# A decoder layer on one core: rows of empty expert slots left out, one result row per token and choice, longer weight runs, another order of the gate product, and a combine without gathers

## The chip, the cores and the metric

The kernel runs on one core of a Trainium2 chip. Its engines are TensorE (PE, with its weight loads as PEld), VectorE (DVE), ScalarE (ACT), GpSimd (POOL) and SyncE (SP). SP, ACT and POOL each issue DMAs on a queue of their own, and the packets of all queues share 16 DMA engines. The metric is the device time of one execution in microseconds (us), the median of several.

## The reference

One layer of a decoder for 1,024 prompt tokens and 32 sample tokens (8 sequences of 4), D = 1024, everything in float32: a mixer (attention and retention) that the change touches in two small places only, then a mixture of experts, then a last normalization. The part that matters, cut short:

```python
def hierarchical_moe(xn, ...):
    ...
    # top group of 4, then the two best of its 8 experts: 2 choices a token
    y = grouped_expert_mlp(xf, experts, gates, w_gate, w_up, w_down)

def run_block(args):              # one expert, 128 slots
    tok, e = args
    xb = x_pad[tok]
    hb = jax.nn.silu(xb @ w_gate[e]) * (xb @ w_up[e])
    return hb @ w_down[e]
...
y = zeros.at[slot_tok].add(yb * slot_gate[:, None])
x = x + y                         # then the final RMSNorm
```

There are 32 experts with 512 hidden channels; w_gate and w_up are 1024 x 512 each, w_down is 512 x 1024. 1,056 tokens times 2 choices are 2,112 rows, 66 an expert on average. With these inputs the fullest expert has 86 and the emptiest 52.

## The kernel before

The work runs in stages one after the other: norm, kv, attention, branch, retention, merge, out, route, experts, beyond, combine. Each stage is a block in which every engine runs its own program; the programs meet through semaphores.

**Products.** A float32 product is made of three fast ones (`split_matmuls`, L148 to L150): each operand is split into a high part H (written by ACT as a copy) and a low part L (raw minus H, written by DVE). So every weight of an expert is loaded once as raw, passed over once by ACT and once by DVE, and used three times by PE.

**Out (L1500 on).** Token tiles of 128 (9 tiles, the last has 32 rows): projection, residual add, normalization `xn` (L1601), stores of x2 and xn2 to DRAM, transposes, router logits.

**Route (L1668 on).** DVE computes for each token and choice a slot: expert e owns slots 128 e to 128 e + 127, with an overflow area behind them. POOL then scatters the token numbers into the table `toktab` (L1829, 18 indirect DMAs). The table was filled with zeros before, so an empty slot names token 0.

**Experts (L1848 to L2073).** One pass for each of the 32 experts, each with 128 slots whether they are filled or not. In pass e the engines work in this order:

- SP loads weights in chunks of 512 KB, four to a matrix: down of e, gate and up of e+2, each as soon as DVE has split the chunk that was there before. A gate or up chunk takes two k tiles of the matrix, so a partition reads two runs of 2 KB.
- POOL: reads the slot table of e+1 into `idx` (L1901, a plain DMA), waits for it, gathers 128 rows of xn2 (L1904, indirect DMA). It waits first until PE has transposed the rows of e.
- ACT: Hd(e-1), hH(e-1) (the hidden rows), Hg(e+1), xH(e+1) (the token rows), sigmoid of the gate product, Hu(e+1), one half of y(e-1) (L1943). Then it waits for both halves of y and issues the store of y to its slots in `y_d` (L1947), a plain DMA of 512 KB.
- DVE: Ld(e-1), hL(e-1), Lg(e+1), xL(e+1), then in `hidden` the gate product G times sigmoid (L1991) and that times U (L1994), Lu(e+1), the other half of y(e-1) (L1999).
- PE: gate product of e (waits for `h_done`, the second product of `hidden` of e-1), transposes of the hidden rows of e-1, up product of e, transposes of the token rows of e+1, down product of e-1.

H, L and raw have one buffer a matrix, as have `rows`, h and y. The last expert has no expert behind it: its down weights are loaded, split and used after all else.

**Beyond (L2076 on).** Handles experts with more than 128 rows; with these inputs its loops run zero times.

**Combine (L2180 on).** For each token tile POOL gathers the two result rows of every token from `y_d` by slot (L2206, 18 indirect DMAs, 4 tile buffers), SP loads x2 (the first four tiles already in the experts' stage), DVE adds gate0 times row0 and x2 (L2234), then gate1 times row1 (L2236), ACT squares and sums, DVE normalizes (L2248), ACT issues the store. `y_d` has slots that nobody writes; the attention stage fills its overflow area with zeros (L501, 4 DMAs of 2 MB on SP's queue, from a tile that POOL clears at L517).

## Time and profile before

| | us |
|---|---|
| median of 3 runs | 2231.74 (2229.24 to 2233.09) |
| span of the profiled execution | 2235.5 |
| experts' stage, first slot table to last y issued | 1519.4 to 2169.9 of the span |
| combine, first issue to the end | 2179.9 to 2235.5 |

For the profiled execution the page gives its span and no other time. PE is busy 86% of the span, DVE 50%, ACT 37%; in the experts' stage the DMA engines are shown at 90% and more in every slice. In rows of a timeline the columns are the start, the duration, the engine (a q behind it means its sequencer, which only issues or waits), the line, the operation, out<-in, the count, and in brackets the idle time of the engine before it with what the profile takes to have ended it.

### The profile page before, as it was taken

To read this page: it belongs to the slowest core of one execution; us is meant where nothing else is said; L and a number is where in the kernel's file an instruction comes from. 1 tells how busy PE (TensorE), PEld (TensorE's weight loads), DVE (VectorE), ACT (ScalarE), POOL (GpSimd) and SP (SyncE) were. 2 spreads that over 40 slices of the span, in tenths; PEclk is the share of its full clock that TensorE was granted. 3 is DMA by queue.
4 is the path that set the end of the run, shared out by engine and by line. 5 is a ranking of instruction groups with operands and counts; after the bars stand their busy time and mean duration, and the time that the engine had idled before them with its cause. 6 is when DMAs were issued, how large, how long until landed. Compare 5 with 4: busy or idle time off the path is not lost. (4 is left out here: it accounts for less than half of the span.)

```text
span 2235.5 us, 29402 instructions
## 1 busy us (share of the span) xinstructions
PE 1912.0 (86%) x9758; PEld 1610.0 (72%) x9758; DVE 1118.4 (50%) x1737; ACT 836.0 (37%) x1481; POOL 305.5 (14%) x412
## 2 busy tenths in 40 slices
PE   6888888799999799999997969915999999999960
PEld 4676666489999788888886968714877777777750
DVE  5024444531110243434334443264888988888856
ACT  5133343431111122222212121113766777666642
POOL 2011111200000030303031000021110110001103
PEclk9998898899999899989897989957999999999985
DMA  6532022122221302111102443254999999999947
GB/s 191 62 100 66 19 66 63 31 77 76 76 75 49 112 20 63 33 59 38 48 31 79 134 127 126 87 194 146 370 370 373 378 376 372 378 373 366 377 174 282
DMA packets 224934, 359.78 MB, mean 161 GB/s; under 512 B 32064, under 2 KB 115056, under 8 KB 224848
## 3 DMA queue, kind: packets, MB, share of 16 engines
q1 hardware_dynamic: 200560, 276.67, 36.6%
q0 software_dynamic: 18512, 61.29, 7.8%
q10 hardware_dynamic: 5808, 21.11, 2.3%
q8 instruction: 32, 0.52, 0.1%
q14 instruction: 22, 0.18, 0.0%
HBM read 304.02 MB, written 57.05 MB: 162 GB/s over the span
## 5 line engine op out<-in xcount | busy, mean ns | idle before, releaser
L1924 ACT ACTIVATE e_Hd<-e_rawd 128x1024 fp32r<-128x1024 f32 x128 | 125.0, 1047 | 167.8 <-DVE e_y L1999 164.8
L1973 DVE TENSOR_TENSOR e_Ld<-e_rawd,e_Hd 128x1024 fp32r<-128x1024 f32 x128 | 148.2, 1221 | 64.0 <-ACT e_Hd L1924 64.0
L1973 DVE TENSOR_TENSOR e_Lg<-e_rawg,e_Hg 128x1024 fp32r<-128x1024 f32 x124 | 143.6, 1219 | 6.2 <-ACT e_Hg L1924 6.2
L1973 DVE TENSOR_TENSOR e_Lu<-e_rawu,e_Hu 128x1024 fp32r<-128x1024 f32 x124 | 143.3, 1219 | 0.0
L148 PE MATMUL bank<-e_Hg,e_xH 128*128 128x512 f32 x256 | 106.0, 414 | 40.7 <-DVE e_hs L1994 37.1
L148 PE MATMUL bank<-r_wH,xH 128*128 128x512 f32 (+1 forms) x288 | 121.4, 422 | 6.3 <-DVE r_wL L1177 3.6
L1924 ACT ACTIVATE e_Hg<-e_rawg 128x1024 fp32r<-128x1024 f32 x124 | 121.0, 1047 | 6.3 <-PE bank L150 6.3
L1924 ACT ACTIVATE e_Hu<-e_rawu 128x1024 fp32r<-128x1024 f32 x124 | 121.0, 1065 | 0.0
L150 PE MATMUL bank<-r_wH,xL 128*128 128x512 f32 (+1 forms) x288 | 115.9, 402 | 0.0
L149 PE MATMUL bank<-r_wL,xH 128*128 128x512 f32 (+1 forms) x288 | 115.7, 402 | 0.0
L148 PE MATMUL bank<-e_Hd,e_hH 128*128 128x512 f32 x256 | 104.6, 409 | 7.3 <-DVE e_hL L1984 7.2
L148 PE MATMUL bank<-e_Hu,e_xH 128*128 128x512 f32 x256 | 103.9, 406 | 0.0
L939 DVE TENSOR_TENSOR b_wL<-raw,b_wH 128x1024 fp32r<-128x1024 f32 x24 | 29.2, 1222 | 148.4 <-ACT b_wH L912 148.4
L149 PE MATMUL bank<-e_Lg,e_xH 128*128 128x512 f32 x256 | 103.0, 403 | 0.0
L150 PE MATMUL bank<-e_Hg,e_xL 128*128 128x512 f32 x256 | 103.0, 402 | 0.0
L150 PE MATMUL bank<-e_Hd,e_hL 128*128 128x512 f32 x256 | 101.7, 397 | 0.0
L149 PE MATMUL bank<-e_Ld,e_hH 128*128 128x512 f32 x256 | 101.7, 397 | 0.0
L150 PE MATMUL bank<-e_Hu,e_xL 128*128 128x512 f32 x256 | 101.3, 396 | 0.0
L149 PE MATMUL bank<-e_Lu,e_xH 128*128 128x512 f32 x256 | 101.2, 395 | 0.0
L782 PE MATMUL bank<-a_PT,a_Vd 128*128 128x512 f32 x120 | 73.2, 737 | 27.2 <-ACT a_PT L600 25.8
L148 PEld LDWEIGHTS bank<-e_Hg,e_xH 128*128 128x128 f32 x256 | 49.2, 192 | 63.9 <-issue 51.6
L524 POOL TENSOR_TENSOR a_S<-a_S,a_rcp 128x1024 f32<-128x1024 f32 (+1 forms) x32 | 57.1, 1786 | 273.6 <-DVE a_rcp L661 273.6
(359 smaller groups left out, 4653.4 us busy)
## 6 DMA issues: line engine op xcount, KB each, us to landing
e_rawg<-in_w_gate SPq DMA_DIRECT2D x128, 512.0 KB, 6.3
e_rawu<-in_w_up SPq DMA_DIRECT2D x128, 512.0 KB, 7.2
e_rawd<-in_w_down SPq DMA_DIRECT2D x128, 512.0 KB, 6.0
raw<-in_w_in SPq DMA_DIRECT2D x51, 512.0 KB, 3.9
y_d<-e_y ACTq DMA_DIRECT2D x32, 512.0 KB, 7.0
y_d<-a_zeros_t SPq DMA_DIRECT2D x4, 2048.0 KB, 9.0
gate_t<-b_gr_s POOLq DMA_DIRECT2D x8, 528.0 KB, 2.9
m_t<-b_m_s POOLq DMA_DIRECT2D x8, 528.0 KB, 3.5
```

The source lines that it names most:

```text
L148: pe.matmul(out, lh, rh, start=first, stop=False)
L149: pe.matmul(out, lh, rl, start=False, stop=False)
L150: return pe.matmul(out, ll, rh, start=False, stop=last)
L524: pool.tensor_tensor(S[:, n % 2, :, w], S[:, n % 2, :, w], rcp[:, n % 2, :].rearrange("p (g o) -> p g o", o=1).broadcast_to([P, GQA, w.sto ...
L782: mm = pe.matmul(banks[6][:], Vd[:, n - 1 + kb].rearrange("p o d -> p (o d)"), PT[:, kb].rearrange("p g i -> p (g i)"), start=(kb == (0 if ...
L939: dve.tensor_tensor(wL[:, q], raw[:, q], wH[:, q].bitcast(F32), ALU.subtract).then_inc(lo_done, 1)
L1924: act.activation(H[kind][:, q], raw[kind][:, q], ACT.Copy).then_inc(w_hi[kind], 1)
L1973: dve.tensor_tensor(L[kind][:, q], raw[kind][:, q], H[kind][:, q].bitcast(F32), ALU.subtract).then_inc(w_lo[kind], 1)
```

## The change

- `toktab` has two numbers a slot: the token, and 2 x token + choice. It is filled with 65,536 (`NOBODY`) instead of zeros.
- The gather of token rows has `bounds_check` T-1 and the result is written by POOL with an indirect DMA (scatter) to row 2 x token + choice of a `y_d` of 2,112 rows, with `bounds_check` 2T-1. A slot with 65,536 is out of bounds in both and is left out. ACT no longer issues the store.
- POOL's program is written out for 32 experts. Slot tables have 8 buffers and are read two experts ahead. For e the order is: table of e+2, gather of e+1, scatter of e-1.
- The columns of xn2 are stored in another order (`by_k`), so that a partition's rows of w_gate and w_up are contiguous in DRAM: one run of 4 KB a chunk instead of two of 2 KB. The router's weights are read in the same order.
- ACT computes the sigmoid ahead of xH, DVE the gate product ahead of xL; PE's gate product waits for the gate product of DVE only (`mul`), and for `h_done` ahead of the up product.
- The last expert's down weights go into the gate buffers, which come free earlier, and are split there behind the gate weights' last use.
- All nine x2 tiles are loaded in the experts' stage. Combine loads 1 MB a tile from `y_d` contiguously on SP's queue, all nine issued at once; ACT multiplies row0 by gate0, POOL adds x2, DVE adds gate1 times row1; SP issues the stores behind the loads, with three output buffers.
- The zero fill in the attention stage is gone. POOL clears the tile `rows` once at the start of experts and of beyond.

```diff
@@ stage_norm .. stage_out
-                sp.wait_ge(zeros_done, 1)
-                    sp.dma_start(ch.y_d[ds(c * Y_ROWS + NE * P, Y_ROWS), :]..., zeros[:]...).then_inc(y_zeroed, 16)
-                sp.wait_ge(y_zeroed, 16 * KVH)
-                pool.memset(zeros[:], 0.0).then_inc(zeros_done, 1)
...
-                    dve.scalar_tensor_tensor(out=xn[0:m, s], in0=x2[0:m, s], scalar=stat[0:m, s, 3:4], in1=gain[0:m],
-                                             op0=ALU.mult, op1=ALU.mult).then_inc(xn_done, 1)
+                    by_k = lambda ap: ap.rearrange("p (m k) -> p k m", k=KT)
+                    dve.scalar_tensor_tensor(out=xn[0:m, s].rearrange("p (k m) -> p k m", k=KT), in0=by_k(x2[0:m, s]), scalar=stat[0:m, s, 3:4],
+                                             in1=by_k(gain[0:m]), op0=ALU.mult, op1=ALU.mult).then_inc(xn_done, 1)
@@ expert_chunk
-        sp.dma_start(dst.rearrange("p (k n) -> p k n", k=2), w[:, 2 * q:2 * q + 2, :]).then_inc(ch.e_w_in[kind][q], 16)
+        src = w.rearrange("o (p k) n -> p (o k n)", p=P)[:, q * 1024:(q + 1) * 1024]
+    sp.dma_start(dst, src).then_inc(ch.e_w_in[into or kind][q], 16)
@@ stage_experts, SP
+                    if left == 1:
+
+                        for q in range(NQ):
+                            sp.wait_ge(w_lo["g"], LAST * NQ + q + 1)
+                            expert_chunk(sp, ch, "d", LAST, q, into="g")
@@ stage_experts, POOL
+                def slots_in(e):
+                    if e >= IDX:
+                        pool.wait_ge(y_st, 16 * (e - IDX + 1))
+                    pool.dma_start(idx[:, e % IDX], ch.toktab[e * P:(e + 1) * P, :]).then_inc(idx_in[e % IDX], 16)
...
+                    pool.indirect_dma_start(out=rows[:], out_offset=None, in_=ch.xn2_d,
+                                            in_offset=bass.IndirectOffsetOnAxis(ap=idx[:, e % IDX, 0:1], axis=0),
+                                            bounds_check=T - 1, oob_is_err=False).then_inc(rows_in, 16)
+
+                def scatter(e):
+                    pool.wait_ge(y_a, e + 1)
+                    pool.wait_ge(y_b, e + 1)
+                    pool.indirect_dma_start(out=ch.y_d, out_offset=bass.IndirectOffsetOnAxis(ap=idx[:, e % IDX, 1:2], axis=0),
+                                            in_=y[:], in_offset=None, bounds_check=2 * T - 1, oob_is_err=False).then_inc(y_st, 16)
...
+                for e in range(NE):
+                    if e + 2 < NE:
+                        slots_in(e + 2)
+                    if e + 1 < NE:
+                        gather(e + 1)
+                    if e >= 1:
+                        scatter(e - 1)
@@ stage_experts, ACT (out_evac, body)
-                    act.wait_ge(y_a, e + 1)
-                    act.wait_ge(y_b, e + 1)
-                    apart(act, ch)
-                    act.dma_start(ch.y_d[ds(e * P, P), :], y[:]).then_inc(y_st, 16)
...
-                        rows_hi(e + 1)
                     gate_sigmoid(e)
                     if left >= 1:
+                        rows_hi(e + 1)
                         split_hi("u", e + 1)
@@ stage_experts, DVE (body)
                         split_lo("g", e + 1)
+                    gate_product(e)
+                    if left >= 1:
                         rows_lo(e + 1)
                     hidden(e)
@@ stage_experts, PE (body)
-                    pe.wait_ge(h_done, e)
+                    pe.wait_ge(mul, e)
                     product("g", G, e)
                     if not first:
                         turn_hidden(e - 1)
+                    pe.wait_ge(h_done, e)
                     product("u", U, e)
@@ stage_combine
+                    sp.dma_start(Y[0:m, t], ch.y_d[2 * t * P:2 * (t * P + m), :].rearrange("(p k) d -> p k d", k=2)).then_inc(y_in[t], 16)
...
+                    pool.tensor_tensor(x2[0:m, t], x2[0:m, t], Y[0:m, t, 0], ALU.add).then_inc(x_sum, 1)
...
+                    act.activation(Y[0:m, t, 0], Y[0:m, t, 0], ACT.Copy, scale=ch.gates[0:m, t, 0:1]).then_inc(y0_done, 1)
...
+                    dve.scalar_tensor_tensor(out=Y[0:m, t, 1], in0=Y[0:m, t, 1], scalar=ch.gates[0:m, t, 1:2], in1=x2[0:m, t],
+                                             op0=ALU.mult, op1=ALU.add).then_inc(a_done, 1)
```

DVE's program for one pass, in the pass that is written out ahead of the last. Names: e_L, e_H and e_raw with g, u, d are the parts of the gate, up and down weights, e_xL the low part of the token rows, e_hL of the hidden rows, e_hs the hidden rows, e_sg the sigmoid. Before:

```order
L1973 TENSOR_TENSOR e_Ld<-e_rawd,e_Hd 128x1024 x4
L1984 TENSOR_TENSOR e_hL<-bank,e_hH 128x512
L1973 TENSOR_TENSOR e_Lg<-e_rawg,e_Hg 128x1024 x4
L1979 TENSOR_TENSOR e_xL<-bank,e_xH 128x512 x2
L1991 TENSOR_TENSOR e_hs<-bank,e_sg 128x512
L1994 TENSOR_TENSOR e_hs<-bank,e_hs 128x512
L1973 TENSOR_TENSOR e_Lu<-e_rawu,e_Hu 128x1024 x4
L1999 COPY e_y<-bank 128x512
```

The same pass in the change:

```order
L1987 TENSOR_TENSOR e_Ld<-e_rawd,e_Hd 128x1024 x4
L1998 TENSOR_TENSOR e_hL<-bank,e_hH 128x512
L1987 TENSOR_TENSOR e_Lg<-e_rawg,e_Hg 128x1024 x4
L2005 TENSOR_TENSOR e_hs<-bank,e_sg 128x512
L1993 TENSOR_TENSOR e_xL<-bank,e_xH 128x512 x2
L2011 TENSOR_TENSOR e_hs<-bank,e_hs 128x512
L1987 TENSOR_TENSOR e_Lu<-e_rawu,e_Hu 128x1024 x4
L2016 COPY e_y<-bank 128x512
```

The gate product moved ahead of the two e_xL; nothing else did, and y is last in both.

ACT's program from the split of the up weights to the next pass, at the loop's end. Before:

```order
L1924 ACTIVATE e_Hu<-e_rawu 128x1024 x4
L1941 REGISTER_ALU
L1943 ACTIVATE e_y<-bank 128x512
L1947 ISA
L1947 DMA y_d<-e_y 128x1024
L1872 REGISTER_ALU
L1872 COMPARE_AND_BRANCH
L1924 ACTIVATE e_Hd<-e_rawd 128x1024 x4
```

In the change:

```order
L1940 ACTIVATE e_Hu<-e_rawu 128x1024 x4
L1957 REGISTER_ALU
L1959 ACTIVATE e_y<-bank 128x512
L1867 REGISTER_ALU
L1867 COMPARE_AND_BRANCH
L1940 ACTIVATE e_Hd<-e_rawd 128x1024 x4
```

The store between e_y and e_Hd, and the wait for DVE's half of y that it had, are gone from ACT.

POOL's program of the experts' stage at its start. Before:

```order
L1911 MEMSET e_idxs 128x1
L1901 DMA e_idxs<-toktab 128x1
L1904 DMA e_rowss<-xn_d,e_idxs 128x1024
L1901 DMA e_idxs<-toktab 128x1
L1904 DMA e_rowss<-xn_d,e_idxs 128x1024
```

In the change:

```order
L1918 MEMSET e_idxs 128x16
L1919 MEMSET e_rowss 128x1024
L1902 DMA e_idxs<-toktab 128x2
L1908 DMA e_rowss<-xn_d,e_idxs 128x1024
L1902 DMA e_idxs<-toktab 128x2 x2
L1908 DMA e_rowss<-xn_d,e_idxs 128x1024
L1902 DMA e_idxs<-toktab 128x2
L1908 DMA e_rowss<-xn_d,e_idxs 128x1024
L1915 DMA y_d<-e_y,e_idxs 2112x1024
L1902 DMA e_idxs<-toktab 128x2
L1908 DMA e_rowss<-xn_d,e_idxs 128x1024
```

The scatter of y (L1915) now stands on POOL between two gathers, with a table read behind it.

## Rows read from the trace of the kernel before

**Rows 1.** The page: its first line.
```profile
span 2235.5 us, 29402 instructions
```

**Rows 2.** Busy time by stretch: stretch, us, the engines, granted clock, DMA share, GB/s.
```profile
1690.00:1725.00 35.00, 32.45 (x152) 25.92 (x151) 30.55 (x33) 27.81 (x34) 2.57 (x4) 1.00 1.01 373
1757.00:1758.00 1.00, 1.00 (x6) 0.78 (x6) 1.00 (x2) 1.00 (x2) 0.29 (x1) 1.00 1.04 426
```

**Rows 3.** Waits, 1480 to 2176 us: who waited for whom, total, times, longest.
```profile
ACT e_Hd L1924 <- DVE e_y L1999: 164.8, 30, 5.8
...
DVE e_Ld L1973 <- ACT e_Hd L1924: 64.0, 31, 2.2
```

**Rows 4.** Timeline of one pass in the experts' loop, several engines.
```profile
1743.90 4.62 DVE L1973 TENSOR_TENSOR e_Lu<-e_rawu,e_Hu 128x1024 fp32r<-128x1024 f32 x4
1744.31 1.66 POOL L1904 DMA_INDIRECT e_rowss<-xn_d,e_idxs  x1 [5.65 <-DMA e_idxs<-toktab]
...
1745.14 3.78 SPq L1845 DMA_DIRECT2D e_rawu<-in_w_up  x4
...
1748.44 0.69 DVE L1999 COPY e_y<-bank 128x512 f32<-128x512 f32 x1
...
1749.36 0.34 ACTq L1947 DMA_DIRECT2D y_d<-e_y  x1
...
1750.13 3.91 ACT L1924 ACTIVATE e_Hd<-e_rawd 128x1024 fp32r<-128x1024 f32 x4 [5.73 <-DVE e_y L1999]
...
1751.22 4.63 DVE L1973 TENSOR_TENSOR e_Ld<-e_rawd,e_Hd 128x1024 fp32r<-128x1024 f32 x4 [2.10 <-ACT e_Hd L1924]
...
1755.93 1.04 PE L2046 MATMUL bank<-identity,e_rowss 128*128 128x128 f32 x8
...
1757.71 0.57 POOL L1901 DMA_DIRECT2D e_idxs<-toktab  x1 [11.75 <-PE bank L2046]
...
1758.21 1.06 ACT L1929 ACTIVATE e_xH<-bank 128x512 fp32r<-128x512 f32 x2
...
1759.64 3.90 ACT L1924 ACTIVATE e_Hu<-e_rawu 128x1024 fp32r<-128x1024 f32 x4
...
1760.91 1.28 DVE L1979 TENSOR_TENSOR e_xL<-bank,e_xH 128x512 fp32r<-128x512 f32 x2
...
1762.92 0.69 DVE L1994 TENSOR_TENSOR e_hs<-bank,e_hs 128x512 f32<-128x512 f32 x1
...
1763.52 0.98 POOL L1904 DMA_INDIRECT e_rowss<-xn_d,e_idxs  x1 [5.25 <-DMA e_idxs<-toktab]
1763.53 4.65 DVE L1973 TENSOR_TENSOR e_Lu<-e_rawu,e_Hu 128x1024 fp32r<-128x1024 f32 x4
1763.85 0.50 PE L148 MATMUL bank<-e_Hg,e_xH 128*128 128x512 f32 x1 [1.28 <-DVE e_hs L1994]
```

**Rows 5.** The instructions on e_rawu: time from issue to landing.
```profile
DMA to landing us min/median/max: 3.6/7.2/11.0
```

**Rows 6.** The instructions on e_rowss: ns min/median/max; time from issue to landing.
```profile
L1904 POOL DMA_INDIRECT e_rowss<-xn_d,e_idxs x32: 976/1620/2022, 1522.5 to 2117.1; - x32
...
DMA to landing us min/median/max: 4.3/7.2/9.5
```

**Rows 7.** The instructions of L1994: count, ns, first and last start.
```profile
L1994 DVE TENSOR_TENSOR e_hs<-bank,e_hs x32: 690/692/692, 1549.1 to 2149.0; 128x512 f32<-128x512 f32 x32
```

**Rows 8.** Timeline from the last expert's store to the end of combine.
```profile
2169.90 0.34 ACTq L1947 DMA_DIRECT2D y_d<-e_y  x1
...
2179.91 0.34 SPq L2193 DMA_DIRECT2D c_gains<-in_norm_final  x1
...
2231.88 1.27 DVE L2248 SCALAR_TENSOR_TENSOR c_os<-c_Y,c_stat,c_gains 32x1024 f32<-32x1024 f32 x1
```

**Rows 9.** The instructions of L524 in the attention stage: ns min/median/max.
```profile
L524 POOL TENSOR_TENSOR a_S<-a_S,a_rcp x32: 1038/1892/1899, 140.4 to 445.3; 128x1024 f32<-128x1024 f32 x28, 128x512 f32<-128x512 f32 x4
```

**Rows 10.** The instructions of L627 in the attention stage: ns min/median/max.
```profile
L627 DVE TENSOR_TENSOR a_wL<-raw,a_wH x8: 1208/1222/1596, 104.7 to 316.1; 128x1024 fp32r<-128x1024 f32 x8
```

More of the change, by code:

```diff
@@ L136, in constants @@
     c["iota"] = np.broadcast_to(np.arange(P, dtype=np.float32), (P, P)).copy()
-    c["tokens"] = (np.arange(NT)[None] * P + np.arange(P)[:, None]).astype(np.int32)
+    token = np.arange(NT)[None] * P + np.arange(P)[:, None]
+    c["tokens"] = np.stack([np.stack([token, 2 * token + k], -1) for k in range(2)], 2).astype(np.int32)
     valid = np.zeros((P, NT), np.float32)
@@ L1885, in body @@
                 def body(e, first, left):
-                    if not first:
+                    if not first and left:
                         load("d", e)
@@ L1913, in _ @@
-                gather(0)
-                walk(pool, body)
+                    if e >= 1:
+                        scatter(e - 1)
+                scatter(LAST)
                 pool.wait_ge(y_st, 16 * NE)
@@ L2201, in _ @@
                 for t in range(NT):
[L2202 to L2207 removed]
+                    m = rows_of(t)
@@ L2224, in _, with first, moments @@
-                for s in range(2):
-                    act.wait_ge(o_st[s], 16 * ((NT + 1 - s) // 2))
+                def first(t):
+                    m = rows_of(t)
+                    act.wait_ge(y_in[t], 16)
+                    act.activation(Y[0:m, t, 0], Y[0:m, t, 0], ACT.Copy, scale=ch.gates[0:m, t, 0:1]).then_inc(y0_done, 1)
+                def moments(t):
+                    m = rows_of(t)
+                    act.wait_ge(a_done, t + 1)
+                    act.activation(junk[0:m], Y[0:m, t, 1], ACT.Square, accum_out=stat[0:m, t, 0:1]).then_inc(sq_done, 1)
+                    act.wait_ge(ms_done, t + 1)
+                    act.activation(stat[0:m, t, 2:3], stat[0:m, t, 1:2], ACT.Sqrt).then_inc(root_done, 1)
@@ L2227, in _ @@
+                first(0)
+                first(1)
+                for t in range(NT):
+                    if t + 2 < NT:
+                        first(t + 2)
+                    moments(t)
             @block.vector
@@ L2355, in hybrid_decoder_layer @@
             stage_out(nc, ch)
-        ch.x2_tiles, ch.x2_in = ch.sbuf(top)("x2_tiles", [P, AHEAD, D]), [ch.sem(f"c_x{s}") for s in range(AHEAD)]
+        ch.x2_tiles, ch.x2_in = ch.sbuf(top)("x2_tiles", [P, NT, D]), ch.sem("c_x")
         with ExitStack() as es:
```

163 lines of the change are left out of this document (76 added, 87 removed).

## The prediction

> **What bounds the kernel now.** I read first where the time goes: the experts' loop is the one stage that the change rebuilds, and it holds most of what can be gained. Its hidden product starts 32 times between 1549.1 and 2149.0 us [rows 7], and two neighbouring passes are 19.63 us apart, from one first split of the up weights to the next (1743.90 to 1763.53) [rows 4]. Three things look like the limit. The DMA engines are at a share of 1.01 with 373 GB/s, DVE is busy 30.6 of 35 us, PE 32.5 [rows 2].
>
> The DMA share misleads. The up weights issued from 1745.14 on land 7.2 us later in the middle and 11.0 at the worst [rows 5], and ACT first touches them at 1759.64, 14.5 us after the issue [rows 4]. Nobody waits for a weight. The loads start when DVE gives a buffer back, so they follow the loop and don't drive it.
>
> What drives it is DVE with one hand-over to ACT. DVE finishes the up split, copies its half of y (1748.44, 0.69 us) and then stands still for 2.10 us until ACT has the first piece of Hd. ACT began that piece at 1750.13, behind the store of y that it issued at 1749.36, for which it had waited 5.7 us in all [rows 4]; over the loop the two waits are 164.8 us and 64.0 us in 30 and 31 passes [rows 3]. The rest of DVE's 19.63 us is work: 17.5. PE stands still 1.28 us a pass, ahead of the gate product, for the hidden product [rows 4].
>
> **The loop, part by part.** (1) The store leaves ACT. ACT no longer waits for DVE's copy, has Hd ready while DVE still splits Lu, and DVE's wait of 2.10 us goes: DVE needs 17.5 us. (2) PE's gate product waits for the first of the two hidden products, which moves ahead of the 1.28 us of xL; DVE is also earlier by (1). PE's wait of 1.28 goes, and PE needs 19.63 - 1.28 = 18.35 us a pass. So PE is late next, and 18.3 is the floor of a pass.
>
> (3) The scatter goes to POOL, between two gathers, and each gather is now queued behind it. This makes a new ring that closes once a pass: PE turns the token rows, and through ACT and DVE comes y, then scatter, table, gather, landing, and the next turning. From the start of the turning: its first half 0.52, two xH 1.06, the second xL 0.7, hidden product 0.69, Lu 4.6, y 0.69, with about 0.4 for six hand-overs 8.7 us [rows 4]. Then POOL: a gather takes 0.98 us when it starts as DVE's split does and 1.66 when a split has run for 0.4 us already (1763.52 and 1744.31) [rows 4], and 0.98 to 2.02 over all [rows 6]. In the new order DVE goes from y straight into Ld, so the scatter meets a running split: I take 2.0. The table read adds 0.57 [rows 4] and POOL pauses 0.2 to 0.3 between two issues; 0.7 in all. The gather lands 7.2 us from its start in the middle, 4.3 at best, 9.5 at worst [rows 6]. Sum: 8.7 + 2.0 + 0.7 + 7.2 = 18.6 us. Half the rows are empty and the weights come in longer runs, which makes the landing shorter; the scatter's rows lie just ahead in the same queue, which makes it longer. I leave 7.2 and take **18.6 us** a pass, 0.3 above PE's floor. Bounds: 18.3 (PE) and, with a landing of 8.0, 19.4.
>
> The Trainium skill (SBUF — State Buffer, Who interferes with whom) says that a VectorE instruction with two SBUF inputs and a GpSimd instruction that reads SBUF block each other. The pair of gathers agrees with it. By it, both the scatter and the gather would be long ones, which is inside the bounds.
>
> (4) The bytes: 12 chunks of 524,288 bytes are 6.29 MB a pass. Rows and y were 1.05 MB more and are 0.54 with 66 of 128 rows. The stretch in which down weights with their 4 KB runs landed shows 426 GB/s [rows 2]; at that rate 6.83 MB take 16.0 us, and at the loop's 373 they take 18.3. Neither is above 18.6, so the saved bytes buy slack and no time. If empty rows were moved all the same, 7.34 MB at 426 take 17.2: no change in the sum either.
>
> (5) Sum of the stage. From the first hidden product (1549.1) to the last y (2169.9) it is 620.8 us [rows 7, 8]. Of the 31 distances between the 32 hidden products (599.9 us), 29 at 19.63 make 569.3, so the first and the last are 30.6 together and the tail is 20.9. After: 29 of 18.6 are 539.4. The first stays. The last is short because no token rows are turned ahead of the last hidden product; now that product otherwise trails PE's up product by 7.0 us (1755.93 to 1762.92) [rows 4], later only by 2.8, so the last distance shrinks less and the two are 33.2. Then the tail. In the tail the last down weights wait in the gate buffers already. From the last up product: down product of the expert before 5.7 (a third of PE's 18.35 less 1.2 of transposes), turn 0.5, hH 0.6, hL 0.7, down 5.7, its last step 0.4, y 0.7, hand-overs 0.4, 14.7 in all. Sum 587.3, **-33.5**.
>
> **Around the loop.** The last store becomes a scatter: +0.7 (POOL's 0.98 instead of ACTq's 0.34 [rows 4, 8]). Clearing `rows` stands on the path at the start of experts and of beyond: POOL needs 1.89 us to add 1,024 elements a partition [rows 9]; clearing reads nothing, so 0 to 1.9, I take 1.0 each. The xn of the last two token tiles reads with a stride of 32 bytes; from 0 to a second pass of 1.27 [rows 8] each, I take 0.8 in all. The zero fill of 8 MB is hidden under attention: 0, with a gain of 1 at most.
>
> **Combine** takes 53.2 us now, from 2179.91 to the end of the last normalization [rows 8]. After: per tile DVE has two instructions of 1.27 and POOL one add of 1.89 [rows 8, 9]. Do they run beside each other? A split on DVE that takes 1.22 took 1.60 when it met an add on POOL [rows 10], so I let them exclude one another: 4.43 a tile, 9 tiles 39.9. Ahead of that lie 9.8 us: a landing of about 7, as the rows show for 0.5 MB in a busy queue [rows 5], the second tile and ACT's first products. 49.7, so **-3.5**. Bounds: if POOL hides fully, 3.5 a tile and 41.8, -11.4. The other way the stores are queued behind nine loads on SP (8.7 MB at 426 GB/s, 20.4 us) and the fourth tile must wait for the first store; at 22 to 26 us it is about to be due, so this costs 0 to 3.
>
> The skill's rule on SBUF named above says the same of this pair; without it the sum would be 8 us lower.
>
> All: -33.5 + 0.7 + 2.0 + 0.8 - 3.5 = **-33.5**; 2235.5 [rows 1] becomes 2202. That execution lies 3.8 above the median of the runs, and I take the difference over: 2231.7 - 33.5 = **2198**.
>
> **Rivals.** Each us of a pass is worth 29 in the sum.
> A. PE is the bound, 18.3: the gathers land early because half the rows are gone. 2198 - 9 = 2189, and 2181 with combine's better end. For it: landings of 4.3 exist, and there are fewer rows to land. Against it: the middle is 7.2, and both POOL instructions grow when DVE splits [rows 4, 6]. 20%.
> B. The ring is late: landings of 8.0 to 8.2 and two long POOL instructions, 19.0 to 19.6 a pass, 2209 to 2227. 12%. The skill (DMA: Bandwidth & Descriptors, Specifications) gives a limit of about 358 GB/s from HBM a core. By it 6.83 MB take 19.1 us and the time would be 2212, a case of this group; the trace has 373 over 35 us, so I give it 2 of the 12.
> C. Slower than before. No row shows an indirect DMA that checks bounds. If the check costs POOL 1 us an instruction, scatter and gather add 2 us to the ring: 20.6 a pass, 2198 + 58 = 2256. It decides from 19.8 on, which is +1.2 in the ring, 0.6 an instruction. Against it: the plain ones take 0.98 undisturbed. 8%, and 3% for ending beside 2232.
> D. The forecast, 18.4 to 19.0: 2185 to 2209 with combine's bounds. 57%.
>
> **How the numbers follow.** Faster: A, B and D, 0.89. Same (within 0.2%, about what a measurement can tell from no change) 0.03, slower 0.08. The range takes D, nearly all of A (18.3 and -11.4 in combine, with 1 to 3 less around it, is 2177) and most of B: 2177 to 2222.
>
> **What would show it.** Right: passes 18.4 to 19.0 apart; ACT's wait for e_y and DVE's for e_Hd gone; PE's wait ahead of the gate product gone and a short one ahead of the turning of rows, released by the landing of e_rowss; the last up product to the last y in 15 us; POOL's add and DVE's two instructions alternating in combine. Wrong: passes at 18.3 with no wait on e_rowss (A); POOL's indirect DMAs well above 2.0 us (C); PE waiting on splits or weights (then DVE or DMA binds, and (1) or (4) fails); combine at 42 us (the exclusion is wrong).

## The result, and the profile after

| | before | after |
|---|---|---|
| median, us | 2232.41 (2229.24 to 2233.42) | 2265.86 (2259.34 to 2268.86) |
| ratio | | 1.0148, 95% interval 1.0130 to 1.0166 |
| span of the profiled execution | 2235.5 | 2267.2 |

The kernel became 1.5% slower. The forecast was 2198 us with a range of 2177 to 2222, so it was wrong, and wrong in its sign. The difference of the two spans, 31.7 us, lies here. The loop is counted from the first to the last start of the hidden product, 31 passes:

| stretch | before | after | forecast difference | measured |
|---|---|---|---|---|
| start to the first hidden product | 1549.1 | 1540.0 | +1.8 | -9.1 |
| loop | 599.9 | 643.4 | -27.3 | **+43.5** |
| last hidden product to the end of y | 20.8 | 14.0 | -6.2 | -6.8 |
| end of y to combine's first issue | 10.1 | 14.7 | +1.7 | +4.6 |
| combine to the end | 55.6 | 55.2 | -3.5 | -0.4 |

Outside the loop the sum was forecast at -6.2 and is -11.7. The -9.1 ahead of the loop is for the most part no effect of the change: e11_store_on_pool and e13_store_later, which have the kernel before up to the experts' stage, reach their first hidden product at 1546.1 and 1542.4 us. The error is the loop's.

The page of after, first line (beside [rows 1]); and busy time by stretch, in the stretch of [rows 2]: stretch, us, PE, PEld, DVE, ACT, POOL, granted clock, DMA share, GB/s.

```profile
span 2267.2 us, 29210 instructions
```

```profile
1690.00:1725.00 35.00, 32.04 (x145) 25.39 (x143) 31.78 (x32) 24.32 (x29) 6.39 (x6) 1.00 0.94 337
```

In this stretch the clock is at its upper level, 2.4 GHz (1.00), and the DMA engines moved 337 GB/s instead of 373. No engine is full. So somebody waits. Waits of after, 1480 to 2230 us: who waited for whom, total, times, longest (beside [rows 3]).

```profile
POOL y_d L1915 <- DVE e_y L2016: 522.9, 31, 22.9
ACT e_xH L1945 <- PE bank L2068: 160.2, 38, 47.1
PE bank L2068 <- DMA e_rowss<-xn_d,e_idxs: 115.0, 30, 49.4
...
DVE e_Ld L1987 <- ACT e_Hd L1940: 7.9, 10, 0.8
```

ACT's wait for e_y (164.8 us) is no longer in the list, and DVE's for e_Hd has gone from 64.0 to 7.9: terms (1) and (2) came as forecast. In their place PE waits for the landing of e_rowss in 29 passes (49.4 of the 115.0 us is the start), and ACT behind it. The wait of POOL for e_y looks the largest, but POOL has nothing else to do; what counts is what is queued behind it. The timeline of one pass in after, several engines (beside [rows 4]).

```profile
1829.80 1.09 PE L2068 MATMUL bank<-identity,e_rowss 128*128 128x128 f32 x8 [1.94 <-DMA e_rowss<-xn_d,e_idxs]
...
1831.12 1.29 DVE L1993 TENSOR_TENSOR e_xL<-bank,e_xH 128x512 fp32r<-128x512 f32 x2 [2.02 <-ACT e_xH L1945]
...
1832.92 4.62 DVE L1987 TENSOR_TENSOR e_Lu<-e_rawu,e_Hu 128x1024 fp32r<-128x1024 f32 x4
...
1837.46 0.69 DVE L2016 COPY e_y<-bank 128x512 f32<-128x512 f32 x1
...
1839.01 1.21 POOL L1915 DMA_INDIRECT y_d<-e_y,e_idxs  x1 [16.77 <-DVE e_y L2016]
...
1840.21 0.60 POOL L1902 DMA_DIRECT2D e_idxs<-toktab  x1
1841.11 1.40 POOL L1908 DMA_INDIRECT e_rowss<-xn_d,e_idxs  x1 [0.30 <-issue]
...
1849.70 1.09 PE L2068 MATMUL bank<-identity,e_rowss 128*128 128x128 f32 x8 [1.57 <-DMA e_rowss<-xn_d,e_idxs]
```

This is the ring that the prediction described: turning, y, scatter, table, gather, turning, here 19.9 us. And the instructions on e_rowss and on e_y in after (ns min/median/max; issue to landing), beside [rows 6]: first the gather, then the scatter.

```profile
L1908 POOL DMA_INDIRECT e_rowss<-xn_d,e_idxs x32: 1042/1396/4248, 1516.0 to 2155.8; - x32
...
DMA to landing us min/median/max: 4.2/8.8/10.5
```

```profile
L1915 POOL DMA_INDIRECT y_d<-e_y,e_idxs x32: 984/1213/4585, 1563.3 to 2198.2; - x32
...
DMA to landing us min/median/max: 3.2/7.9/11.6
```

Passes (from one start of L2011 to the next) are 19.7 to 22.8 us over most of the loop, 22.0 to 26.1 in three at its start; 21.06 in the mean of the 29 between the first and the last.

They are of two kinds. Two stretches of 8 us in after, each from the start of a turning on, columns as above:

```profile
1725.53:1733.53 8.00, 8.00 (x39) 6.64 (x40) 6.68 (x8) 6.15 (x8) 0.00 (x0) 1.00 0.85 319
1746.11:1754.11 8.00, 8.00 (x32) 6.58 (x33) 6.43 (x7) 4.87 (x6) 0.00 (x0) 0.79 0.82 301
```

In the second the granted clock falls to 1.2 GHz for a part of the time, and PE comes through 32 matmuls instead of 39. The scatters of these two passes:

```profile
1734.74 1.21 POOL L1915 DMA_INDIRECT y_d<-e_y,e_idxs  x1 [16.69 <-DVE e_y L2016]
1756.02 2.04 POOL L1915 DMA_INDIRECT y_d<-e_y,e_idxs  x1 [17.78 <-DVE e_y L2016]
```

The down product ends 8.2 us from the start of the turning instead of 6.7, y later by 0.7, and the scatter is long. Counted from turning to turning, 19 of the 30 passes of after have the upper level throughout and take 20.13 us (median); 11 have a part at the lower and take 22.11. Ahead of each fall in the loop PE had stood still for the rows, 1.8 us or more; waits as long stand in passes without a fall too. In e1_swap below, where PE doesn't wait, the view shows 1.00 from 1600 to 2090 us, and 0.97 in after from 1600 to 2170.

### The profile page after: what moved, and what is told of

It is laid out like the page before. It is cut to its first block and busy times, and to the rows that moved or that the text cites. A ratio compares the mean times of both kernels' runs of the same rounds, so it can differ in the third digit from the quotient of the medians.

```text
span 2267.2 us, 29210 instructions
## 1 busy us (share of the span) xinstructions
PE 1918.2 (85%) x9758; PEld 1617.7 (71%) x9758; DVE 1133.8 (50%) x1728; ACT 851.6 (38%) x1490; POOL 361.4 (16%) x436
## 5 line engine op out<-in xcount | busy, mean ns | idle before, releaser
L1987 DVE TENSOR_TENSOR e_Lg<-e_rawg,e_Hg 128x1024 fp32r<-128x1024 f32 x128 | 148.4, 1220 | 13.1 <-ACT e_Hg L1940 13.1
L1987 DVE TENSOR_TENSOR e_Ld<-e_rawd,e_Hd 128x1024 fp32r<-128x1024 f32 x124 | 143.6, 1220 | 7.9 <-ACT e_Hd L1940 7.9
L2068 PE MATMUL bank<-identity,e_rowss 128*128 128x128 f32 x256 | 39.6, 305 | 115.0 <-DMA e_rowss<-xn_d,e_idxs 115.0
L1915 POOL DMA_INDIRECT y_d<-e_y,e_idxs x32 | 49.6, 1549 | 540.1 <-DVE e_y L2016 522.9
L2068 PEld LDWEIGHTS bank<-identity,e_rowss 128*128 128x128 f32 x256 | 31.4, 154 | 128.6 <-issue 76.1
```

What stands on the lines that cost most here:

```text
L1915: pool.indirect_dma_start(out=ch.y_d, out_offset=bass.IndirectOffsetOnAxis(ap=idx[:, e % IDX, 1:2], axis=0), in_=y[:], in_offset=None, bou ...
L1987: dve.tensor_tensor(L[kind][:, q], raw[kind][:, q], H[kind][:, q].bitcast(F32), ALU.subtract).then_inc(w_lo[kind], 1)
L2068: tr = pe.transpose(XT[b][:, k * P:(k + 1) * P], rows[:, (4 * b + k) * P:(4 * b + k + 1) * P], ch.ident[:])
```

## The experiments

All are measured against the kernel before on the same chip. A gather's place in the ring is given as the median of 26 passes, counted from the start of the turning.

**1. The ring opened.** One place in POOL's order:

```diff
                         gather(e + 1)
-                    if e >= 1:
-                        scatter(e - 1)
+                    if e >= 2:
+                        scatter(e - 2)
+                scatter(LAST - 1)
                 scatter(LAST)
```

> The changed kernel with one thing moved: on POOL the gather of the next expert's rows stands ahead of the scatter of y instead of behind it (gather e+1, scatter e-2, where it was gather e+1, scatter e-1 of the pass). Theory R (the ring turning of rows, xH, xL, hidden product, Lu, y, scatter, gather, landing sets the 20.75 us of a pass): the ring is cut, PE's wait for e_rowss (115 us) goes, a pass takes 18.3 to 18.6, the time is 2266 minus 29 times 2.3, about 2195 to 2205. Rival D (the DMA engines can't deliver 6.8 MB faster, and the late rows are only how that shows): a pass stays above 20, PE waits for weight splits in place of rows, the time stays above 2245. Rival P (POOL's indirect DMAs with a bounds check are slow by themselves): like D, with POOL late.

2183.6 us, ratio 0.9785 (0.9758 to 0.9812). This one place turns 1.5% slower into 2.1% faster. Timeline of POOL in e1_swap, one pass:

```profile
1829.90 1.04 POOL L1908 DMA_INDIRECT e_rowss<-xn_d,e_idxs  x1 [8.98 <-PE bank L2069]
1837.29 1.17 POOL L1915 DMA_INDIRECT y_d<-e_y,e_idxs  x1 [6.35 <-DVE e_y L2017]
1838.45 0.59 POOL L1902 DMA_DIRECT2D e_idxs<-toktab  x1
1848.02 1.03 POOL L1908 DMA_INDIRECT e_rowss<-xn_d,e_idxs  x1 [8.98 <-PE bank L2069]
```

The gather now starts 1.8 us after the start of the turning and is released by it, its rows are there at 8.6, and PE needs them at 18.12. Busy time by stretch in e1_swap, columns as above:

```profile
1690.00:1725.00 35.00, 35.00 (x164) 28.58 (x164) 33.57 (x36) 28.07 (x34) 5.57 (x6) 1.00 1.00 380
```

PE is busy in all 35 us; passes are 18.12 us. The floor that the prediction put at 18.35 is 18.12. R is right, D (the transfers can't keep up) falls. The time is 11 us below what R was given: R took 2.3 us off a pass, and the mean pass fell by 3.0 (21.06 to 18.05), the slow clock's part with it.

**2. What the ring is made of.** Three runs on the changed kernel, scatter still between two gathers. e9_table_late reads the table behind the gather:

```diff
-                    if e + 2 < NE:
-                        slots_in(e + 2)
                     if e + 1 < NE:
                         gather(e + 1)
+                    if e + 2 < NE:
+                        slots_in(e + 2)
```

> The changed kernel with the read of the slot table behind the gather instead of ahead of it; the scatter stays where it was, between two gathers. Theory R (the ring y, scatter, gather, landing, turning sets the pass): the table read and its pause, 0.6 to 0.9 us, leave the ring, passes fall from 20.6 to 19.8 to 20.1 us, and the time to 2241 to 2250. Rival (the gather's packets wait behind others whenever it is issued): the landing comes at the same time as before, passes stay at 20.5 to 20.7, 2262 to 2270.

2251.9 us (2246.8 to 2256.9), passes 20.05 in the middle and 20.46 in the mean (after: 20.64, 21.06). The passes are R's and the time is 2 us above R's range, but R's reason carries little of it. POOL in e9_table_late:

```profile
1848.68 1.19 POOL L1915 DMA_INDIRECT y_d<-e_y,e_idxs  x1 [15.92 <-DVE e_y L2016]
1850.18 2.00 POOL L1908 DMA_INDIRECT e_rowss<-xn_d,e_idxs  x1 [0.31 <-issue]
```

The gather starts 0.6 earlier from the turning than in after (10.7 and 11.3 us) and takes 2.00 instead of 1.40; it ends at the same moment, 12.7. Passes at the upper clock take 20.02 from turning to turning where after has 20.13. The rest of the gain is that only 4 of 30 passes have a part at the lower clock instead of 11. Taking an instruction out of a ring doesn't give back its length when the next one grows.

e10_plain_store puts a plain DMA of 66 rows in the scatter's place, so the results stand where combine doesn't look for them:

```diff
-                    pool.indirect_dma_start(out=ch.y_d, out_offset=..., in_=y[:], in_offset=None, ...).then_inc(y_st, 16)
+                    pool.dma_start(ch.y_d[66 * e:66 * e + 66, :], y[0:66, :]).then_inc(y_st, 16)
```

> The changed kernel, but POOL writes the first 66 rows of y to 66 rows of y_d of each expert with a plain DMA, in the scatter's place; the result rows then lie in other places than combine reads. As many bytes, as many rows, no indices. Theory Q (what lies ahead in POOL's queue costs the gather's landing 2 us whatever it is): only the shorter issue counts, 0.6 to 0.9 us less a pass, 19.7 to 20.0, 2237 to 2246. Rival I (the indices themselves make the scatter slow to start, and the gather behind it): the landing falls from 8.8 to about 6.8 us as well, passes of 18.1 to 18.4, 2185 to 2197.

2200.8 us, passes 18.5. Q, by which it doesn't matter what lies ahead, is wrong, since the passes are 1.2 us below its range; I is 4 us off in the time, and the landing fell to 8.1 and not to 6.8. e14_no_scatter leaves the scatters out and keeps the wait; four plain DMAs behind the last expert fill y_d:

```diff
                     pool.wait_ge(y_b, e + 1)
-                    pool.indirect_dma_start(out=ch.y_d, ...).then_inc(y_st, 16)
+                    if e < LAST:
+                        pool.sem_inc(y_st, 16)
+                        return
+                    for b in range(4):
+                        pool.dma_start(ch.y_d[528 * b:528 * b + 528, :]..., y[0:66]...).then_inc(y_fin, 16)
```

> The changed kernel without the 31 scatters inside the loop: POOL still waits for y of e-1 at the same place between two gathers, but issues nothing there; behind the last expert four plain DMAs write the last expert's y over all rows of y_d, so the results are left out. The ring then is turning, y (8.35), hand-over, table read and pause (about 1.5), gather's landing. Theory Q (the rows of y that lie ahead in POOL's queue delay the gather's landing): the landing, counted from the gather's start, falls from 8.8 us to 6.5 to 7.2, the ring to 16.5 to 17.2, and PE sets passes of 18.1. Rival H (it is the time in the pass: at that moment SP's queue is full of weight packets whatever lies ahead): the landing stays at 8.2 to 9.0; the ring is then 18.2 to 19.0, and PE still waits a little for e_rowss.

2244.1 us, of which some 46 are the four DMAs at the end (last y at 2123.2, combine at 2184.2; 14.7 us apart in after). The loop has passes of 18.26 in the middle, 18.53 in the mean. Timeline of POOL, and time from issue to landing of e_rowss, in e14_no_scatter:

```profile
1842.42 0.56 POOL L1903 DMA_DIRECT2D e_idxs<-toktab  x1 [15.91 <-POOLq L1917]
1843.28 1.80 POOL L1909 DMA_INDIRECT e_rowss<-xn_d,e_idxs  x1 [0.30 <-issue]
...
DMA to landing us min/median/max: 4.3/8.3/10.3
```

The same line in e1_swap and in e10_plain_store:

```profile
DMA to landing us min/median/max: 4.3/6.7/8.3
```

```profile
DMA to landing us min/median/max: 4.2/8.1/9.8
```

Set apart into the instruction and what follows its end (medians of the 26 passes; the start is counted from the start of the turning, the pass from hidden product to hidden product):

| | gather's start | gather issue | its end to landing | passes |
|---|---|---|---|---|
| before: alone, its table long landed | 7.7 | 1.6 | 5.7 | 19.63 |
| e1_swap: alone, its table long landed | 1.8 | 1.0 | 5.7 | 18.12 |
| e14_no_scatter: a table read ahead | 9.8 | 1.8 | 6.6 | 18.26 |
| e10_plain_store: 66 plain rows and a table read ahead | 10.35 | 1.25 | 6.8 | 18.52 |
| after: 66 scattered rows and a table read ahead | 11.3 | 1.4 | 7.4 | 20.64 |

By the ranges on record H holds in e14_no_scatter: the landing is 8.3 us from the gather's start (H: 8.2 to 9.0, Q: 6.5 to 7.2) and the pass 18.26. Of the 2.1 us by which the gather of after lands later from its start than that of e1_swap, 0.4 is a longer issue, 0.9 is there without the scatter, and 0.8 comes with it, of which 66 plain rows make only 0.2. The Trainium skill (DMA: Bandwidth & Descriptors, Two DMAs through the same engine are not ordered) says that within one queue of one DMA engine descriptors start in order. That the gather lands later with rows ahead agrees with it; that scattered rows cost more than as many plain ones is not explained by it. The 0.9 stays open: e14_no_scatter has the table read right ahead of the gather, so it doesn't part the moment in the pass from the table read.

Counted as a ring, the scatter costs more on POOL than in the landing: from y to the gather's start are 3.0 us in after and 1.4 in e14_no_scatter, and the landing from the start is 8.8 and 8.4 (medians of the same 26 passes). And with no scatter at all, the wait for y still keeps some passes off PE's floor.

The length of the issue follows DVE. DVE's split of e_Ld is four pieces, 1.13 us from start to start. The gather takes 2.0 us when it starts 0.1 us into a piece (e9_table_late), 1.8 at 0.35 (e14_no_scatter), 1.4 at 0.7 (after), 1.25 at 0.9 (e10_plain_store), and the scatter 1.2 at 0.9 and 2.0 at 0.1 (both in after). Beside instructions of DVE that read one operand from the banks it takes 1.04 (e1_swap). So the gather of e9_table_late is no longer because of the scatter ahead of it: that of e14_no_scatter has none and takes 1.8.

**3. Bytes and runs.** e2_runs2k gives the changed kernel the old weight layout (two runs of 2 KB), e3_allrows lets the gather move all 128 rows, e5_swap_runs2k is e2's edit on e1_swap.

```diff
@@ e2_runs2k and e5_swap_runs2k: layout of weights, xn and router as before
-        src = w.rearrange("o (p k) n -> p (o k n)", p=P)[:, q * 1024:(q + 1) * 1024]
+        src = w.rearrange("o (k p) n -> p (o k) n", p=P)[:, 2 * q:2 * q + 2, :]
+        dst = dst.rearrange("p (k n) -> p k n", k=2)
@@ e3_allrows: an empty slot has a token number inside the bounds
+    empty[:, :, 0] = np.arange(P)[None]
```

> The changed kernel with the gate and up weights, the router weights and the columns of xn2 in the order of the kernel before (two runs of 2 KB a partition in a chunk). Theory A (the packets of POOL's queue take turns with those of SP's queue on each DMA engine, so a 4 KB row waits for 4 KB of weights where it waited for 2 KB): scatter and gather land earlier, the gather 1.5 to 2 us sooner than its 8.8 us, a pass takes 19.0 to 19.5 and the time is 2215 to 2235. Rival: the run length plays no part in it, the landing stays at 8.8 and the time at 2266 or, with the stage_out gain lost, a few us above. If 4 KB runs were what the loop lives on, it would be slower than 2280.

> The changed kernel with in-bounds tokens in the empty slots, so that the gather moves all 128 rows again; the scatter still leaves the empty slots out. Theory A and R: 62 rows more in the queue, but if the rows of filled slots sit on few DMA engines (slots are filled from 0 up) the most loaded engine has the same rows as before, and the landing is later by 0 to 1 us, the time 2266 to 2295. Rival S (skipping rows makes the indirect DMA slow): the landing gets shorter than 8.8 us and the time falls below 2255.

> Both edits at once: gather ahead of the scatter and weights in runs of 2 KB. Theory R: with the ring cut the landing of the rows has slack and the run length plays no part; a pass takes 18.3 to 18.8 and the time is within 8 us of the kernel with the gather ahead alone. Rival D: the runs of 2 KB cost DMA time, at 6.8 MB a pass and 373 GB/s 18.3 us, so weights come late and it is over 10 us slower than the kernel with the gather ahead alone.

2256.3 (2254.4 to 2258.3), 2268.0 and 2184.6 us. The old layout in the changed kernel is a little faster (passes 20.30 in the middle; the gather lands in 8.6), less than A asked for: the run length is not the cause. Most of these 10 us are the clock: at the upper level a pass takes 20.05 from turning to turning beside 20.13 in after, but 5 passes have a part at the lower instead of 11. All rows instead of half cost 2 us, within the spread of after; the ring doesn't depend on the row count. In the opened ring the layout makes no difference (1 us), though the up weights land 12.5 us after their issue in e5_swap_runs2k and 5.8 in e1_swap. Long runs bought slack that nobody used.

**4. Which part holds the gain.** e8_old_gate is e1_swap with sigmoid and gate product back behind xH and xL, and PE's gate product waiting for both products.

```diff
                         split_lo("g", e + 1)
-                    gate_product(e)
-                    if left >= 1:
                         rows_lo(e + 1)
+                    gate_product(e)
                     hidden(e)
```

> e1_swap with the old order around the gate product: ACT's sigmoid behind xH, DVE's gate product behind xL, PE's gate product waiting for both hidden products. Theory G0 (the gain came from the store that left ACT; with DVE no longer late, both hidden products end about 4 us after the start of the turning of the rows, before PE has come through its 6.7 us of transposes and down product): passes of 18.1 to 18.6 us, 2184 to 2199, no wait of PE ahead of the gate product. Rival G1 (the order itself carries term (2), 1.28 us a pass): passes of 19.2 to 19.5, 2218 to 2226, with PE waiting for e_hs.

2188.2 us (2185.6 to 2190.7) at passes of 18.12, and a span of 2183.9 beside e1_swap's 2184.1. G0 is right: the new order of the gate product is worth at most 2 us in the whole loop (558.0 us beside 555.8), none of them in its middle.

Then the kernel before with one move, the store of y from ACT to POOL. In e11_store_on_pool it stands behind the gather of the next expert, as the scatter does in the change; in e13_store_later one gather later.

```diff
@@ both: ACT's out_evac
-                    act.wait_ge(y_a, e + 1)
-                    act.wait_ge(y_b, e + 1)
-                    apart(act, ch)
-                    act.dma_start(ch.y_d[ds(e * P, P), :], y[:]).then_inc(y_st, 16)
@@ e11_store_on_pool, POOL's body of pass e
                         gather(e + 1)
+                    if not first:
+                        store(e - 1)
@@ e13_store_later, POOL
+                gather(1)
+                gather(2)
+                with pool.Fori(1, NE - 2) as e:
+                    gather(e + 2)
+                    store(e - 1)
...
```

> The kernel before with one move: the plain store of y is issued by POOL, behind the gather of the rows of the next expert, and no longer by ACT. Nothing else of the change: all 128 rows, 2 KB runs, old order of the gate product, old combine. Theory S (ACT's wait for DVE's half of y was all that held the loop): ACT's wait for e_y and DVE's for e_Hd go, passes fall from 19.6 to 18.1 to 18.3 us, PE waits for nothing, 31 passes give 41 to 46 us, and the time is 2186 to 2192. Rival T (the bytes or the two ends of the loop matter too: fewer rows, longer runs, the last expert's weights in other buffers): passes of 18.6 or more, 2205 and above.

2447.2 us, 1.0961 (1.0935 to 1.0987). I had repeated the change's own mistake: store(e - 1) behind gather(e + 1) is the place of the scatter in the changed kernel, and ahead of gather(e + 2). Here it costs 9.6%, since in the kernel before the gather also waits for its slot table, and that now stands in the ring too. POOL in e11_store_on_pool:

```profile
1840.93 0.55 POOL L1911 DMA_DIRECT2D y_d<-e_y  x1 [17.30 <-DVE e_y L2004]
1842.06 0.54 POOL L1901 DMA_DIRECT2D e_idxs<-toktab  x1 [0.57 <-issue]
1848.33 1.80 POOL L1904 DMA_INDIRECT e_rowss<-xn_d,e_idxs  x1 [5.74 <-DMA e_idxs<-toktab]
...
1868.19 0.56 POOL L1911 DMA_DIRECT2D y_d<-e_y  x1 [18.06 <-DVE e_y L2004]
```

A pass is 27.2 us. PE stands still for 6.2 us ahead of the turning at 1857.10, and from 1855 to 1862 us the view by stretch shows a granted clock of 0.50, 1.2 GHz.

```profile
1855.00:1862.00 7.00, 4.91 (x16) 4.24 (x17) 2.83 (x5) 3.50 (x6) 0.00 (x0) 0.50 0.47 176
```

> As e11_store_on_pool, but POOL's order is gather of the rows of e+2, then store of y of e-1, so that no gather and no slot table is queued behind a y that is not yet there. One place in POOL's order is the only difference. Theory S, kept (ACT's wait for DVE's half of y was what held the loop before; e11_store_on_pool closed the ring y, store, table, gather, turning): passes of 18.1 to 18.3 us, PE waits for nothing, 2186 to 2192. Rival T (fewer rows, longer runs and the other tail of the change are needed for that): passes of 18.6 or more, 2205 and above.

2194.7 us, ratio 0.9835 (0.9815 to 0.9856), between S and T. Passes are 18.09 for the first twelve and then 18.5, mean 18.34. One store moved to the right place gives 37 of the 47 us of e1_swap, but not all: the two rows below, the view by stretch and the waits of e13_store_later, show what binds next.

```profile
1900.00:1950.00 50.00, 49.40 (x227) 39.42 (x226) 46.86 (x49) 40.62 (x48) 5.69 (x8) 1.00 1.04 397
```

```profile
ACT e_Hg L1934 <- DMA e_rawg<-in_w_gate: 48.2, 55, 2.0
```

ACT waits for gate weights, at 397 GB/s. A pass of this kernel moves 6.29 + 1.05 = 7.34 MB, and 7.34 MB at 397 GB/s are 18.5 us, the pass. That division alone proves nothing, since the rate was taken from the same passes; the wait does, and e5_swap_runs2k, which with runs of 2 KB too but 6.83 MB has passes of 18.13 in the mean. So here the transfers bind, and T's half about the bytes is right. The other part of T is the tail: last hidden product to the end of y is 20.7 us here and 14.0 in e1_swap.

**5. Combine.** e6_dve_weigh is e1_swap with both weighted sums on DVE; e12_act_stores lets ACT issue the stores as well.

```diff
@@ e6_dve_weigh, DVE's weigh; POOL's add and ACT's scaling leave
+                    dve.scalar_tensor_tensor(out=Y[0:m, t, 0], in0=Y[0:m, t, 0], scalar=ch.gates[0:m, t, 0:1], in1=x2[0:m, t], ...)
-                    dve.scalar_tensor_tensor(out=Y[0:m, t, 1], ..., in1=x2[0:m, t], ...)
+                    dve.scalar_tensor_tensor(out=Y[0:m, t, 1], ..., in1=Y[0:m, t, 0], ...)
@@ e12_act_stores, ACT's loop over the tiles
                     moments(t)
+                    if t >= 1:
+                        store(t - 1)
```

> The changed kernel with the scatter one place later (as in e1_swap), and in combine both weighted sums on DVE again (gate0 times row0 plus x2, then gate1 times row1), without POOL's add and ACT's scaling. Theory X (POOL's add and DVE's instructions hold each other up: 2.60 us and 3.36 us where alone they take 1.89 and 1.28): a tile then costs DVE three instructions of 1.28 and two small ones, 4.2 to 4.4 us instead of the 5.1 measured, so combine falls from 55.3 us to 46 to 49 and the whole is 6 to 8 us below e1_swap, 2175 to 2178. Rival L (the tiles come in at the rate of the loads, or the chain through ACT's square and root sets the step): the step stays at 5.1 and the time at 2183 to 2185.

> e6_dve_weigh with combine's stores issued by ACT, each behind ACT's square and root of the next tile, instead of by SP behind the nine loads. Theory Q (in e6_dve_weigh DVE stood still 2.5 us once because the first store's packets waited in SP's queue behind 9 MB of loads): that stall goes and the last store starts at the same distance from the last normalization, 2 to 3 us less, 2175 to 2177. Rival: the store is late wherever it is issued, since all packets share the same engines, or ACT's own waits delay the root of the next tile: 2178 to 2181.

2178.6 us and 2177.7 us, ratios 0.9768 (0.9752 to 0.9784) and 0.9752 (0.9732 to 0.9772). Four rows of e1_swap's combine, then two of e6_dve_weigh's:

```profile
2150.07 1.28 DVE L2281 SCALAR_TENSOR_TENSOR c_os<-c_Y,c_stat,c_gains 128x1024 f32<-128x1024 f32 x1
2150.95 2.60 POOL L2241 TENSOR_TENSOR x_tiles<-x_tiles,c_Y 128x1024 f32<-128x1024 f32 x1 [2.50 <-ACT c_Y L2248]
2151.27 3.36 DVE L2269 SCALAR_TENSOR_TENSOR c_Y<-c_Y,gates,x_tiles 128x1024 f32<-128x1024 f32 x1
...
2155.16 1.28 DVE L2281 SCALAR_TENSOR_TENSOR c_os<-c_Y,c_stat,c_gains 128x1024 f32<-128x1024 f32 x1
```

```profile
2144.42 1.28 DVE L2252 SCALAR_TENSOR_TENSOR c_Y<-c_Y,gates,x_tiles 128x1024 f32<-128x1024 f32 x1
...
2154.34 1.28 DVE L2267 SCALAR_TENSOR_TENSOR c_os<-c_Y,c_stat,c_gains 128x1024 f32<-128x1024 f32 x1 [2.49 <-DMA out_y_prompt<-c_os]
```

Beside each other the add takes 2.60 and DVE's instruction 3.36; alone they take 1.89 [rows 9] and 1.28. These lengths hold waiting: from the end of the normalization (2151.35) to the end of the weighting (2154.63) are 3.28 us, the add and the weighting one after the other and 0.1. A tile needs 5.10 us with POOL's help and 4.33 without, which is also the distance of most tiles in the kernel before: X is right in the tile, though combine misses X's 46 to 49 us by the stall below. This agrees with the Trainium skill (SBUF — State Buffer, Who interferes with whom), by which two such instructions lock each other out. The stall of 2.49 us is a store queued behind nine loads on SP's queue, and it is gone in e12_act_stores: combine is 50.8 us with it and 48.4 without, as Q said. The whole moved by less than its spread (2173.6 to 2178.5), so the two totals alone don't tell them apart. e12_act_stores is 2.5% faster than the kernel before and 3.9% faster than the change.

## Why the prediction was wrong

**The step that failed is term (3), the length of the ring,** and in it above all the landing. The mechanism was right: the prediction named this ring, that PE would wait for e_rowss, and that it decides from 19.8 us on. What it had not at all is what PE's waits do to the clock.

| from the start of the turning | forecast | after, median |
|---|---|---|
| y complete | 8.7 | 8.35 |
| y complete to the scatter's start | 0 | 0.86 |
| scatter's issue | 2.0 | 1.2 |
| table read and pauses | 0.7 | 0.9 |
| gather's start to its landing | 7.2 | 8.8 |
| landing to turning | 0 | 0.12 |
| sum | 18.6 | 20.2 |

The median of these 26 passes is 20.4 and their mean 20.85. In 9 of them the clock falls, y ends 0.7 later, and the scatter starts at the beginning of a piece of DVE's split instead of near its end and takes the 2.0 us forecast. 2.46 us more than 18.6 in each of 29 passes are 71 us; the loop was forecast at -27.3 and came at +43.5, 70.8 apart. An estimate from the two kinds of pass parts them. 30 passes of 20.13 instead of 18.6 are 46 us: the ring at the upper clock. The 11 passes with a part at the lower clock take 28 us more than as many of 20.13, 7 of them in the first alone, in which PE also stands still for 9.2 us; the other 19 are 5 us below. So without the falls of the clock the kernel would still have been slower than before, by a quarter to a half of a percent and not by 1.5% (an estimate).

Three things went wrong in the ring. The landing of 7.2 was the median of gathers that start 7.7 us from the turning and have POOL's queue to themselves. The prediction named both opposing effects (fewer rows, scatter ahead) and let them cancel without a row; the bound of 8.0 had no row either, though [rows 6] had 9.5. Half the rows bought nothing (e3_allrows). Then the 0.86 between y and the scatter was missing, a hand-over to POOL that was not taken over from anywhere. And a ring that is a median of 18.6 against a floor of 18.3 has no slack, so each late landing is paid in full and no early one is given back. To this comes the clock: the sum has 18.6 us for every pass, as if PE's matmuls kept their speed whatever PE waits.

**Terms (1) and (2)** hold as to waits that go (164.8 us gone, 64.0 to 7.9), and PE's floor is 18.12 instead of 18.35. But (2) gave the new order of the gate product a share in it, and e8_old_gate shows that it has none: PE waited only because DVE was late.

**Term (4)**, bytes buy no time, is right in the changed kernel (e3_allrows), and so is the stand against a limit of 358 GB/s: 380 and 397 GB/s were held. No run moves all rows in the opened ring. The term is wrong as a general statement, since e13_store_later is bound by its 7.34 MB. The 426 GB/s of one microsecond [rows 2] was never held. The Trainium skill (Perfetto Trace Analysis, Engine Utilization) gives the 16 engines some 435 GB/s and calls 120% of 358 the practical ceiling of a core alone; the highest that a stretch of 50 us shows here is 398 (e13_store_later, 1584 to 1634 us).

**Term (5)**: the tail of 14.7 came at 14.0. **Around the loop**: the way from the last y to combine was forecast at +1.7 and is +4.6. POOL's row for the clearing in beyond and its wait, in after:

```profile
2198.19 0.98 POOL L1915 DMA_INDIRECT y_d<-e_y,e_idxs  x1 [6.75 <-DVE e_y L2016]
2209.71 0.10 POOL L2149 MEMSET v_idx_s<- 128x2 int32 x1 [10.54 <-POOLq L1872]
2209.74 0.95 POOL L2150 MEMSET v_rows_s<- 128x1024 f32 x1
```

The clearing takes 0.95 as taken; the rest is 10.5 us between the scatter's end and POOL's next instruction, which no row of before had suggested. The stage out is no longer than before (139.9 us against 144.4), so the strided xn costs nothing visible. The attention stage was 346.0 us after 350.8, but without the zero fill it lies anywhere from 343.7 to 350.2 in other traces here; whether the fill cost anything was not settled.

**Combine**: the exclusion is real and they take turns, as forecast. The 4.43 us a tile had 1.27 twice and 1.89 and nothing for what lies between: 0.53 us of small instructions (scaling of the mean, root, reciprocal) ahead of the normalization, in which POOL has nothing to add yet, and 0.1 of hand-over. A tile took 5.10, first issue to last normalization 52.8 instead of 49.7, and -3.5 became -0.4. The bound with POOL hidden was also added up a little wrong: 9 tiles of 3.5 and 9.8 are 41.3, not 41.8.

**The rivals.** A's floor was reached as soon as the ring was open. B was the right rival and ended at 19.6 where the truth was 21. C named 2256 and the deciding point of 19.8, both close, but by another mechanism: the bounds check costs nothing to speak of (the scatter's issue is 1.2, a gather's 1.04 undisturbed with it and 0.98 without). The chances were the second error: the forecast lay 1.2 us from the point at which the sign turns, two of the ring's terms were carried over from another situation, and 8% for a slower kernel was far too little.

## What to carry to other kernels

When an in-order engine gets a new wait between two prefetches, write down what stands behind it and whether the awaited thing depends on it: if so, it is a ring, and its landing must be taken from the late end of the rows, not the middle, because it pays late and never earns early. Moving the waiting instruction one prefetch later (the scatter of e-2 instead of e-1) cost nothing and was worth 82 us here. Where the new wait falls on PE, look at the granted clock of every pass and not of one stretch: a mean and a median that lie apart are its sign, and a small edit can gain by it alone. An engine that helps out with an add is no help if its instruction and the other's lock each other out.

## What the runs showed of the hardware that was not expected

- The issue of an indirect DMA on POOL is as long as DVE's split lets it be: 1.04 us beside reads from the banks, and 1.2 to 2.0 beside a split of e_Ld, the longer the less of the running piece is over when it starts.
- Two gathers alone in their queue land 5.7 us after their issue ends, whether they start 1.8 or 7.7 us from the turning (e1_swap, before); with a table read right ahead, 9.8 us from the turning, it is 6.6 (e14_no_scatter).
- 66 rows stored plainly ahead of a gather delay its landing by 0.2 us, 66 scattered ones by 0.8.
- In after the granted clock fell to 1.2 GHz in 11 of 30 passes, each time after PE had stood still for its rows; in e1_swap in none.
- The DMA engines held 397 GB/s over the loop of e13_store_later, for one core.
- From the end of the last store of y to POOL's next instruction it is 10.5 us when POOL issues it as a scatter, 10.7 when POOL issues it plainly (e10_plain_store, e11_store_on_pool, e13_store_later), and 8.0 when ACT does (before, 2170.2 to 2178.2).
- Rows left out by a bounds check shortened the landing by 0.3 us: 8.8 us with 66 rows and 9.1 with 128.
